# Fourth tile of a dense block moved into the norm's accumulators, residual sums in pairs with the column weight on ScalarE, tokens loaded by halves, last stage shared between engines

## The reference

```
h = rmsnorm(x, norm_mix_pre);  z = h @ w_in          # 1024 -> latents and HGRN2 parts
mix = [attention heads | HGRN2 heads] @ w_out
x = x + rmsnorm(mix, norm_mix_post)
h = rmsnorm(x, norm_ffn_pre);  u = h @ w_ffn_up      # gate and value, 2 x 2816
f = (silu(conv3(gate)) * value) @ w_ffn_down
x = x + rmsnorm(f, norm_ffn_post)
```

## Time and profile before

| | |
|---|---|
| median of 3 runs | 2124.92 us (2124.26 to 2130.24) |
| the profiled execution | 2126.35 us |
| its span, first to last instruction | 2124.5 us |
| busy | PE 94%, DVE 54%, ACT 35%, POOL 6% |
| mean granted TensorE clock | 0.955 of full |
| DMA | 141.85 MB, mean 67 GB/s |

### The profile page before, as it was taken

How to read it: one execution, slowest core, us unless ns; L and a number is a source line. 1 busy time by engine, 2 the same in 40 slices (tenths; PEclk the granted TensorE clock), 3 DMA queues, 4 the chain that set the end, 5 groups by cost and what they waited for, 6 DMA issues and landing times.

```text
span 2124.5 us, 30928 instructions
## 1 busy us (share of the span) xinstructions
PE 1989.3 (94%) x12316; PEld 1800.7 (85%) x12316; DVE 1152.5 (54%) x1967; ACT 739.5 (35%) x1166; POOL 117.7 (6%) x113
## 2 busy tenths in 40 slices
PE   6999989899899999999989999898998999999996
PEld 6989866469799999999888888664797999999995
DVE  4677764332666515664556777452237664166636
ACT  5444434333522222222353444352245222222222
POOL 0000033300000000000000001232000000000000
PEclk9999988889999999999999998797999999999998
DMA  4211130131122222222121111302211222222211
GB/s 168 70 52 62 57 86 2 45 110 50 34 80 80 70 73 68 79 80 70 50 93 42 52 61 60 72 1 79 75 62 52 70 80 70 72 70 78 80 60 55
DMA packets 43198, 141.85 MB, mean 67 GB/s; under 512 B 5088, under 2 KB 9056, under 8 KB 43040
## 3 DMA queue, kind: packets, MB, share of 16 engines
q1 hardware_dynamic: 33248, 117.51, 16.9%
q10 hardware_dynamic: 9808, 22.37, 3.3%
HBM read 130.13 MB, written 8.65 MB: 65 GB/s over the span
## 4 chain that ended last, share of the span: by engine, by line
PE 79%; DVE 11%; ACT 8%; issue 2%; DMA 1%; ACTq 0%; DVEq 0%; SPq 0%
PE G L381 61%; PE WA L381 8%; PE WB L381 6%; DVE Y L1272 1%; PE G L385 1%; DVE tmp L1272 1%; DVE wlo L1272 1%; DVE DE L1272 1%; PE WB L385 1%; ACT sq L864 1%; DVE X L1272 1%; ACT whi L864 1%; ACT Y L864 1%; DVE Z L1272 1%; ACT R L864 1%
## 5 line engine op out<-in xcount | busy, mean ns | idle before, releaser
L381 PE MATMUL G<-Hh,wlo 128*128 128x328 f32 x2240 | 723.4, 323 | 50.7 <-DVE Hl L1272 22.1
L381 PE MATMUL G<-Hh,whi 128*128 128x328 f32 x2240 | 710.0, 317 | 0.0
L381 PE MATMUL G<-Hl,whi 128*128 128x328 f32 x2240 | 703.9, 314 | 0.0
L381 PEld LDWEIGHTS G<-Hh,wlo 128*128 128x128 f32 x2240 | 428.8, 191 | 69.4 <-DVE Hl L1272 26.9
L381 PEld LDWEIGHTS G<-Hh,whi 128*128 128x128 f32 x2240 | 428.2, 191 | 1.1 <-issue 0.2
L381 PEld LDWEIGHTS G<-Hl,whi 128*128 128x128 f32 x2240 | 428.4, 191 | 0.0
L864 ACT ACTIVATE whi<-wraw 128x1024 fp32r<-128x1024 f32 x192 | 203.6, 1061 | 547.0 <-PE G L381 525.5
L1272 DVE TENSOR_TENSOR wlo<-wraw,whi 128x1024 fp32r<-128x1024 f32 x192 | 235.3, 1226 | 236.7 <-ACT whi L864 228.3
L381 PE MATMUL G<-gh,wlo 128*128 128x328 f32 x704 | 220.3, 313 | 3.5 <-issue 3.5
L381 PE MATMUL G<-gl,whi 128*128 128x328 f32 x704 | 220.4, 313 | 0.0
L381 PE MATMUL G<-gh,whi 128*128 128x328 f32 x704 | 219.6, 312 | 0.0
(11 more groups left out here) (212 smaller groups left out, 2445.3 us busy)
## 6 DMA issues: line engine op xcount, KB each, us to landing
wraw<-in_wstream SPq DMA_DIRECT2D x192, 512.0 KB, 3.3
ckT<-in_ckT SPq DMA_DIRECT2D x12, 512.0 KB, 4.3
ctok<-in_ctok SPq DMA_DIRECT2D x12, 512.0 KB, 3.4
S<-in_s ACTq DMA_DIRECT2D x8, 512.0 KB, 5.4
o_sst<-S ACTq DMA_DIRECT2D x8, 512.0 KB, 3.3
o_y<-Y ACTq DMA_DIRECT2D x16, 164.0 KB, 1.8
ckT<-in_ckT ACTq DMA_DIRECT2D x4, 512.0 KB, 4.2
ctok<-in_ctok ACTq DMA_DIRECT2D x4, 512.0 KB, 4.0
```

What stands on the lines that cost most here:

```text
L381: return pe.matmul(out, lhsT, rhs, start=start, stop=stop, skip_group_check=True)
```

## The change

- **Fourth tile.** Tile 3 of the blocks that follow a norm lies in WA, the accumulator of the norm's sums. TensorE waits for `R` ("rstd") before it. Its weights are split earlier: on ScalarE before `rstd_pre`, on VectorE at the end of the half-1 work; at the gated block's first unit that split is gone. `tile_free` looks back for the last tile that used the same accumulator.
- **Residual.** `residual(x, k, n)` does n = 2 blocks in one instruction (blocks 0 and 1 of a half still alone), as `tmp = Y*R` with R broadcast over the blocks and `X = X + tmp`, both tensor_tensor. "x" rises by n at the end of it. `rest(x, k)` (the Hl) of both blocks follows the pair. The column weight is applied by ScalarE: in the copy out of the accumulator for the mixer (`out_copy`), in a copy of its own for the gated block (one for each of 6 tiles, four half ones).
- **Order in half 0.** `out_b`, `norm_sum`, `rstd_post_b` and `ffn_out_b` stand at other blocks; one weight split is moved from half 0 to half 1.
- **Start.** `X` comes in 16 transfers by halves, with half 0 first; piece 1 stands after one of them in SyncE's queue, the constants behind piece 2. The first square waits for `ones` alone. ScalarE loads the Ln/Exp table at once and computes the sigmoids of the lower bounds by Exp, with an addition and reciprocal on VectorE; the mask constants are made between the Hl of half 1.
- **End.** VectorE makes 12 of the 16 half blocks as six pairs of `X*R`, ScalarE scales these 12 by the final weight, VectorE does four as before; SyncE's queue sends all. R of half 0 is made while half 1 of the residual runs.

The diff, cut to what the prediction speaks of and with 8 columns of indentation taken off:

```diff
@@ -175,7 +175,8 @@
...
 def PS(tt):
-    return WB if tt % TILES in (2, T_UP[0] + 2) else G[tt % 2]
+    i = tt % TILES
+    return WB if i in (2, T_UP[0] + 2) else WA if i in (3, T_UP[0] + 3) else G[tt % 2]
...
@@ -306,12 +311,23 @@
...
         if g == 0:
-            for k in range(1, KD, 2):
-                sp.dma_start(X[:, k, :], a["xT"][k]).then_inc(S(f"x_in{k}"), 16)
+            x_in(0, 1)
         if g == 1:
-            for t_, name in ((ones, "ones"), (ident, "ident"), (mask_f, "masks"), (reset_f, "reset"),
+            sp.dma_start(ones[:, :], a["ones"]).then_inc(S("ones"), 16)
+            for x, k in ((0, 3), (0, 5), (0, 7), (1, 1), (1, 3), (1, 5), (1, 7)):
+                x_in(x, k)
+        if g == 2:
+            for t_, name in ((ident, "ident"), (mask_f, "masks"), (reset_f, "reset"),
                              (rope, "rope"), (ind_f, "ind")):
                 sp.dma_start(t_[:, :] if len(t_.shape) == 2 else t_[:, :, :], a[name]).then_inc(S("const"), 16)
+    for k in range(KD):
+        sp.wait_ge(S("y_scaled"), k + 1)
+        sp.dma_start(a["o_y"][k, :, cols_of(0)], Y[:, k, cols_of(0)]).then_inc(S("out"), 16)
+    for i in range(KD // 2):
+        sp.wait_ge(S("y_scaled"), KD + i + 1)
+        sp.dma_start(a["o_y"][i, :, cols_of(1)], Y[:, i, cols_of(1)]).then_inc(S("out"), 16)
+        sp.wait_ge(S("y_out"), i + 1)
+        sp.dma_start(a["o_y"][KD // 2 + i, :, cols_of(1)], Y[:, KD // 2 + i, cols_of(1)]).then_inc(S("out"), 16)
...
@@ -412,8 +428,11 @@
...
     def tile_free(tt):
-        if tt >= 2:
-            pe.wait_ge(S(f"evac{tt % 2}"), slot_use(tt) - 1)
+        last = tt - 2
+        while last >= 0 and PS(last) is not G[tt % 2]:
+            last -= 2
+        if last >= 0 and PS(tt) is G[tt % 2]:
+            pe.wait_ge(S(f"evac{tt % 2}"), slot_use(last))
...
@@ -681,12 +700,15 @@
...
         def sum_ffn_out(x, k):
-            if l and not x and k == 6:
+            if l and not x and k == 5:
                 norm_sum(n0 - N_NORM + N_FFNPOST, WA)
...
         first_two(t0, g0, l * SPLITS, 2 * l, ("y2a", 2 * l) if l else None, sum_ffn_out)
+        pe.wait_ge(S("rstd"), n0 + N_MIXPRE + 1)
         for i in range(3, 6):
             in_tile(l, i)
+        if not l:
+            pe.wait_ge(S("const"), 16 * N_CONST)
...
@@ -821,12 +843,14 @@
...
         def sum_mix_out(x, k):
-            if not x and k == 5:
+            if not x and k == 3:
                 norm_sum(n0 + N_MIXPOST, WA)
...
         for hf in range(2):
             for i in range(2 * FH):
+                if not hf and i == 3:
+                    pe.wait_ge(S("rstd"), n0 + N_FFNPRE + 1)
                 if hf or i >= 3:
                     tile(t0 + T_UP[hf] + i, [(g0 + P_UP[hf] + i, k * P, k) for k in range(KD)], Hh, Hl)
...
@@ -867,13 +891,16 @@
...
     act.dma_start(cols[:, :, :], a["cols"]).then_inc(S("cols_in"), 16)
-    for k in range(0, KD, 2):
-        act.dma_start(X[:, k, :], a["xT"][k]).then_inc(S(f"x_in{k}"), 16)
+    for x in range(2):
+        for k in range(0, KD, 2):
+            act.dma_start(X[:, k, cols_of(x)], a["xT"][k, :, cols_of(x)]).then_inc(S(f"x{x}_in{k}"), 16)
...
+    exp_table()
     act.wait_ge(S("cols_in"), 16)
...
@@ -944,17 +971,17 @@
...
         if l == 0:
+            act.wait_ge(S("lbd"), 1)
+            did(f(lbs[:, 1, 0, :], lbs[:, 0, 0, :], ACT.Exp, scale=-1.0), "lb_exp")
+            did(f(lbs[:, 1, 1, :], lbs[:, 0, 0, :], ACT.Exp), "lb_exp")
             w_high(0, 0)
             for x in range(2):
                 for k in range(KD):
-                    act.wait_ge(S(f"x_in{k}"), 16)
+                    act.wait_ge(S(f"x{x}_in{k}"), 16)
                     split_xh(l, 0, C_MIXPRE, x, k)
                     if not x and k in (0, 4):
                         w_high(0, 1 + k // 4)
-            act.wait_ge(S("lbd"), 1)
-            did(f(lbs[:, 1, 0, :], lbs[:, 0, 0, :], ACT.Sigmoid), "lb_sig")
-            did(f(lbs[:, 1, 1, :], lbs[:, 0, 0, :], ACT.Sigmoid, scale=-1.0), "lb_sig")
-        exp_table()
+        w_high(l, SPL)
...
@@ -1141,7 +1168,8 @@
...
-            did(f(two(Y[:, n, :])[:, sl, :], halves(G[tt % 2])[:, sl, :], ACT.Copy), name, None if name == "evac_a" else slot_use(tt))
+            did(f(two(Y[:, n, :])[:, sl, :], halves(G[tt % 2])[:, sl, :], ACT.Copy,
+                  scale=cols[:, l, C_MIXPOST + n:C_MIXPOST + n + 1]), name, None if name == "evac_a" else slot_use(tt))
...
@@ -1172,13 +1200,14 @@
...
                 split_xh(l, 2 * l + 1, C_FFNPRE, x, k)
+                if not x and k == 1:
+                    out_b(KD - 1)
                 if not x and k == 2:
-                    out_b(KD - 1)
-                if not x and k == 3:
                     w_high(l, P_UP[0] + 2)
-                if not x and k == KD - 2:
+                if not x and k == 4:
                     rstd_post_b(2 * l + 1)
         act.dma_start(cst[:, :], a["cst"][l]).then_inc(S("cst_in"), 16)
+        w_high(l, P_UP[0] + 3)
         rstd_pre(2 * l + 1)
...
@@ -1208,12 +1238,20 @@
...
                     square_x(n0 + N_FFNPOST, n, Y[:, n, :])
+                    step(f(Y[:, n, :], Y[:, n, :], ACT.Copy, scale=cols[:, l, C_FFNPOST + n:C_FFNPOST + n + 1]))
...
             did(f(sq[:, c % 2, cols_of(0)], Y[:, n, cols_of(0)], ACT.Square), "sqa")
+            scale_y(n, 0)
...
@@ -1230,24 +1274,25 @@
...
                 if not x and k == 1:
+                    w_high(l + 1, 1)
+                if not x and k == 2:
                     ffn_out_b(KD - 2)
-                if not x and k == 1:
-                    w_high(l + 1, 1)
-                if not x and k == 5:
+                if not x and k == 3:
+                    w_high(l + 1, 2)
+                if not x and k == 4:
                     ffn_out_b(KD - 1)
                 if not x and k == KD - 2:
-                    w_high(l + 1, 2)
-                if not x and k == KD - 1:
                     rstd_post_b(2 * l + 2)
                     act.dma_start(a["o_conv"][l], cout[:, :, :]).then_inc(S("conv_out"), 16)
+                if l + 1 == DEPTH and x and k == 1:
+                    rstd_end(0)
...
-    for x in range(2):
-        act.wait_ge(S("sqh_summed"), 4 * KD * DEPTH + KD * (x + 1))
-        rstd_half(x, "rstd_end")
-    for x in range(2):
-        for k in range(KD):
-            act.wait_ge(S("y_out"), KD * x + k + 1)
-            act.dma_start(a["o_y"][k, :, cols_of(x)], Y[:, k, cols_of(x)]).then_inc(S("out"), 16)
+    rstd_end(1)
+    for i in range(KD + KD // 2):
+        x, k = divmod(i, KD)
+        act.wait_ge(S("y_raw"), i + 1)
+        did(f(Y[:, k, cols_of(x)], Y[:, k, cols_of(x)], ACT.Copy, scale=cols[:, 0, C_FIN + k:C_FIN + k + 1]),
+            "y_scaled")
...
@@ -1324,15 +1369,14 @@
...
-    def residual_half(l, c_w, x, then):
-
-        for k in range(KD + 1):
-            if k < KD:
-                t_ = tmp[:, k % 2, cols_of(x)]
-                step(tt_(t_, Y[:, k, cols_of(x)], R[:, cols_of(x)], ALU.mult))
-                did(stt(X[:, k, cols_of(x)], t_, col(l, c_w + k), X[:, k, cols_of(x)], ALU.mult, ALU.add), "x")
-            if k:
-                then(x, k - 1)
+    def spread(x, n):
+        return R[:, cols_of(x)].rearrange("p (a n) -> p a n", a=1).broadcast_to([P, n, HALF])
+
+    def residual(x, k, n=1):
+
+        t_, xs = tmp[:, 0:n, cols_of(x)], X[:, k:k + n, cols_of(x)]
+        step(tt_(t_, Y[:, k:k + n, cols_of(x)], spread(x, n), ALU.mult))
+        did(tt_(xs, xs, t_, ALU.add), "x", by=n)
...
@@ -1656,21 +1710,37 @@
...
-        def rest_for_ffn(x, k):
+        def rest(x, k):
...
-        residual_half(l, C_MIXPOST, 0, rest_for_ffn)
+
+        residual(0, 0)
+        residual(0, 1)
+        w_low(l, P_UP[0] + 1)
+        rest(0, 0)
+        rest(0, 1)
+        residual(0, 2, 2)
+        add_square_b(n0 + N_MIXPOST, KD - 2)
+        rest(0, 2)
+        rest(0, 3)
+        residual(0, 4, 2)
+        add_square_b(n0 + N_MIXPOST, KD - 1)
+        rest(0, 4)
+        rest(0, 5)
+        residual(0, 6, 2)
+        rest(0, 6)
+        rest(0, 7)
         dve.wait_ge(S("rstd"), n0 + N_MIXPOST + 1)
         dve.wait_ge(S(f"evac{(t0 + T_OUT + KD - 1) % 2}"), slot_use(t0 + T_OUT + KD - 1))
-        residual_half(l, C_MIXPOST, 1, rest_for_ffn)
+        residual(1, 0)
+        residual(1, 1)
+        rest(1, 0)
+        w_low(l, P_UP[0] + 2)
+        rest(1, 1)
+        for k in range(2, KD, 2):
+            residual(1, k, 2)
+            rest(1, k)
+            rest(1, k + 1)
+        w_low(l, P_UP[0] + 3)
         dve.wait_ge(S("rstd"), n0 + N_FFNPRE + 1)
...
@@ -1739,31 +1810,45 @@
...
+
+        residual(0, 0)
+        residual(0, 1)
+        w_low(l + 1, 0)
+        rest(0, 0)
+        rest(0, 1)
+        w_low(l + 1, 1)
+        residual(0, 2, 2)
+        ffn_out_b(KD - 2)
+        rest(0, 2)
+        rest(0, 3)
+        residual(0, 4, 2)
+        ffn_out_b(KD - 1)
+        rest(0, 4)
+        add_square_b(n0 + N_FFNPOST, KD - 2)
+        rest(0, 5)
```

(23 more changed lines are left out.)

91 lines of the change are left out of this document (44 added, 47 removed).

## The result

The changed kernel takes 2106.59 us (median of 4 runs, 2102.41 to 2108.55) against 2124.59 us of the kernel before beside it (4 runs): ratio 0.991, 95% interval 0.9884 to 0.9935. It is faster, by 18.0 us (0.9%) where 26.6 were forecast (26.3 between the forecast time and the median of before). The profiled execution took 2108.55 us, its span 2106.8 us.

A forecast was written before the change was run, and what follows sets the result against it. TensorE, busy 94% of the span, was taken as the bound; 14.1 + 7.9 - 0.2 + 3.9 + 0.9 = 26.6 us off the profiled 2126.35, and 1.43 for the median, gave 2098.3 us, range 2092 to 2107.

The forecast's parts named there:

- Fourth tile, gated block: Tile 3 of each gated block starts without idle time or lower clock after it: 8.4 us gained, twice.
- It just fits: Gated block: the split for tile 4 ends 9.0 us after R, tile 3 at 9.15, so tile 4 does not wait.
- Fourth tile, mixer's block: Tile 3 of each mixer's block loses 2.37 us idle and 1.46 of lower clock: 3.8 us gained, twice.
- cost 1.35 us: Half 1 of a gated block's residual pass: block 7 starts at S+17.9 instead of S+16.55 because of pairs.
- S = 559.8, as before: S, half 1's start on VectorE, stays put: about 2.9 us saved in half 0 goes into waits for Hh.
- the round: Residual: a pair takes 2 by 0.87 = 1.73 us plus 2.4, so 4.1 to 4.2, or 2.1 a block.
- Between the layers: Stretch between layers: idle before half 1 falls from 2.81 to about 1.4 us; 0.3 us gained after half 1's cost.
- Start: Kernel start: TensorE goes on at 11.65 instead of 15.15 and 0.4 us of constants wait goes: 3.9 us gained.
- Rival 3: Start: halves load at half the rate, so the start gains 0: 2102.5 us; chance 0.08.
- End: Kernel end: last R 0.6 us earlier, 12 copies of 0.60, sends of 0.38: 0.9 us gained, bounds 0 and 2.5.
- Weight copies: Where ScalarE applies the column weight, a copy takes 0.09 us more; 0.2 us lost in all.
- rival 2: Three residual passes: pair handshake waits 20% longer, TensorE drops to lower clock before half 1: 2104 to 2112 us; chance 0.13.

The follow-up runs named there:

- experiment 1: Kernel before with the fourth tile alone (tile 3 in WA, weights split earlier); residual, loads and end as before: 2111.06 us, ratio 0.9908.
- experiment 2: Changed kernel without the fourth tile: tile 3 back in G1, all new orders kept: 2123.74 us, ratio 0.9974.
- Experiment 10: Kernel before with only the early weight split in the mixer's block; tile 3 stays in G1: 2124.27 us, ratio 0.9984.
- experiment 5: Changed kernel with the residual one block at a time, weight on ScalarE and moved split kept: 2095.57 us, ratio 0.9838.
- experiment 8: Changed kernel with single-block residual, split back in half 0, VectorE making all 16 end products, SyncE sending 12, ScalarE 4: 2097.22 us, ratio 0.9855.
- experiment 7: Changed kernel with tokens loaded in 8 transfers of whole blocks, rest of the new start kept: 2111.04 us, ratio 0.9912.
- experiment 4: Changed kernel with the ending of before (16 products on VectorE, 16 sends on ScalarE's queue): 2103.03 us, ratio 0.9884.
- experiment 6: Changed kernel with the moved weight split back in half 0, pairs kept: 2113.09 us, ratio 0.9911.
- experiment 9: Kernel of experiment 8 with tokens loaded by whole blocks: 2101.92 us, ratio 0.9883.

## Why the prediction was right and wrong

- **Fourth tile, gated block: 8.4 forecast, 8.24 and 8.58 measured** (experiment 1); without it the gain goes in full (experiment 2). Right in mechanism and size. "It just fits" missed by 0.23 and 0.33 us (the changed kernel's rows at 588.05 and 1625.79).
- **Fourth tile, mixer's block: 3.8 forecast, 4.1 and 4.2 measured, for another reason.** The step that failed is the cause: I read "released by VectorE's taking of tile 1" and put it down to the accumulator. Experiment 10 gains 3.7 in layer 1 by the place of one split, and experiment 2 keeps all but 0.5 us with tile 3 in G1. The accumulator is worth about 0.5 here. The number came out because the change also moved that split, which I had counted as free and not as the gain. In layer 0 the early split gives only 2.3 on the old start, as the masks and pieces come late there; the new start gives the rest.
- **Pairs: "cost 1.35 us" in half 1 and "S = 559.8, as before" in half 0 were both too low.** Measured from S = 556.60 (`last_two` at 524.46, before 559.77 and 528.50), half 0 is 32.14 - 31.27 = 0.87 us longer. From S to the third tile's end it takes 24.02 us for 22.21, 1.81 more. The term mis-sized is the round: I had 0.87 for each instruction of a pair, and it takes 0.94 to 0.95; every later Hl inherits that. Three pairs of two such instructions make about 0.45 us a half. That is what half 1 missed by (1.81 for 1.35) and half of what half 0 did; in the rest of half 0 are waits of ScalarE for which I had nothing, 0.35 us before R of half 1 and 0.37 before the last Hh. With tile 4's 0.23 this gives 8.4 - 0.87 - 1.81 - 0.23 = 5.5 us, measured 5.59. Between the layers a gain of 0.3 turned into a loss of 0.5; single blocks take the stretch to 58.95 and 59.28 us (experiments 5 and 8), so the cost of the pairs is in it too. I had seen that a pair's round exceeds TensorE's pace; what I had not asked is what single blocks would give with the weight on ScalarE. That is 3.7 us a gated block and 2.6 us between the layers (experiment 5): more than the pairs' visible loss of 0.87 + 1.81. With single blocks and the split where it was, a gated block takes 488.8 us against 489.9 with the column weight on VectorE (experiments 8 and 1); the new places of the half-0 work are in that 1.1 too, and no run tells the two apart. (An estimate from the rows of DVE: each of the eight sums of half 0 takes 0.50 us instead of 0.56, which is about 0.5 of the 1.1.)
- **Start: 3.9 forecast, 2.33 measured.** The 8 issues took 0.58 us each on average (the first four start 0.48 apart as forecast, the later ones 0.50 to 0.88), not 0.48, which with the table and piece 0 behind them put ScalarE's part of piece 1 at 10.02 for 9.2, and tile 1 at 12.39 for 11.65: 2.8 us gained for 3.5. The 0.4 us of the first square came as forecast: from tile 1's first matmul to that of tile 0's next block it is 13.99 - 12.39 = 1.60 us, before 17.16 - 15.15 = 2.01. All of half 0 then runs 3.1 us ahead, and 0.8 of it went before half 1: its first matmul at 26.83 waited 0.63 us, behind 0.8 us of new steps for the lower bounds on VectorE (25.44 to 26.21) that I had counted nowhere. In the window from 4 to 8 us 353 GB/s moved instead of 404. Rival 3 (half the rate) did not come, but its direction holds: the halves lose 1.5 us (experiment 7). They do so through issue time: the rate is 11% lower too (353 for 397), but with halves the split of piece 1 did not wait for its transfer. The Trainium skill ("DMA: Bandwidth & Descriptors", Bandwidth) asks for larger transfers; the runs agree in sign, while half the rate for 164 KB, my estimate from its table, which is for transfers that GpSimd issues, was far too pessimistic here.
- **End: 0.9 forecast, -1.67 measured.** Behind the last R it took 11.8 us for the 10.3 that I had, and this is the changed ending's own cost: copies 0.65 for 0.60 (7.8 us for 7.2), sends 0.50 for 0.38, and 2.5 us from the last send's start for 2.2. R itself came 40.24 us after `last_two` (39.66 before), 0.6 later where 0.6 earlier was forecast. The pairs are not the cause: experiments 2 and 7, with the same pairs, have it at 39.32 and 39.33, and experiments 5 and 8, with single blocks, at 39.38 and 39.37; all four ran at a granted clock of 1.00 there. What differs is the clock of the last square sums. The ten us from 30 us after `last_two` on, first of the changed kernel, then of experiment 2:

```profile
2084.74:2094.74 10.00, 8.52 (x17) 3.80 (x16) 9.02 (x12) 5.32 (x12) 0.00 (x0) 0.66 0.00 0
```

```profile
2104.95:2114.95 10.00, 5.95 (x17) 2.38 (x16) 9.02 (x12) 6.12 (x13) 0.00 (x0) 1.00 0.00 0
```

  VectorE does the same work in the same time, and TensorE needs 8.52 us for 17 matmuls at 0.66 and 5.95 at 1.00. The kernel before and experiments 4 and 6 had 0.83 there, and R at 39.66, 39.60 and 39.87. So about 0.9 us of the loss belong to this execution; at 1.00 the same ending took 51.0 us from `last_two` (experiment 2), 0.6 more than before. R of half 0 is early, but that bought nothing, since its copies stand behind the last R, where I had counted them.
- **Weight copies:** the scaled copy added 0.09 us to `last_two`'s wait (1.60 to 1.69), as said. The Trainium skill ("ScalarE: Activation LUTs", What ACT_TABLE_LOAD costs) gives that for the operand; the trace agrees.
- **The stretch not changed:** level 0 to `last_two` in layer 0 took 454.69 us before, the shortest of the profiles of all twelve kernels (up to 464.67), and 457.09 after. The work was the same, the granted clock not (experiment 9). The kernels of experiments 1 and 10, which also run the code of before there, took 462.94 and 460.46. So this 2.4 us of the miss goes with the clock of single executions, not with the change. What sets the clock there is open; nothing here tried it.

The forecast time was 2098.3; 2106.59 lies at the upper edge of the range and inside rival 2 (2104 to 2112), whose mechanism, the handshake in pairs, is one of four parts of the miss. By the stretches, 2.4 of the 8.9 us missing come from the passes of the gated blocks, 2.6 from the end, 1.6 from the start, 2.3 from the unchanged stretches; the mixer's blocks gave 0.7 more than forecast and the stretch between the layers 0.8 less. Of these, the 2.3 and 0.9 of the end's 2.6 go with the clock and not with a term of the sum.
